# A two-block network on one core: the mixer's q matmuls by pairs of weight units, a stage's banks asked for one by one, and weight splits at fixed steps of a unit

## What is computed

```python
for l in range(DEPTH):
    x = layer_norm(ALPHA * x + 0.5 * swiglu(x, ffn1_w_gu[l], ffn1_w_down[l]), ln1_g[l], ln1_b[l])
    x = layer_norm(ALPHA * x + hybrid_mixer(x, w_in[l], ...), ln2_g[l], ln2_b[l])
    x = layer_norm(ALPHA * x + 0.5 * swiglu(x, ffn2_w_gu[l], ffn2_w_down[l]), ln3_g[l], ln3_b[l])

def hybrid_mixer(x, w_in, ...):
    z = x @ w_in
    sc_b, sc_c, sc_h, q, k, v, cc_a, cc_gate = jnp.split(z, IN_OFFSETS, axis=-1)
    y_sc = sc_b * depthwise_conv(sc_c * sc_h, sc_conv_w)            # 3 taps
    q = rope(q.reshape(b, s, 8, 64), positions)
    k = rope(k.reshape(b, s, 2, 64), positions)
    y_att = banded_window_attention(q, k, v, attn_sink)             # blocks of 128 tokens
    u = depthwise_conv(cc_a * jax.nn.sigmoid(cc_gate), cc_conv_w) + cc_conv_b   # 31 taps
    y_cc = jax.nn.silu(layer_norm(u, cc_ln_g, cc_ln_b))
    return jnp.concatenate([y_sc, y_att, y_cc], axis=-1) @ w_out
```

## Time and profile before

| | |
|---|---|
| median of three runs | 3479.86 us (3476.91 to 3484.40) |
| the profiled execution, its own time | 3478.07 us |
| its span, first to last instruction | 3476.3 us |
| mean granted TensorE clock | 0.986 |
| TensorE busy | 3324.5 us, 96% of the span |
| VectorE busy | 1725.2 us, 50% |
| ScalarE busy | 1097.7 us, 32% |
| weight loads | 514 of 512 KB, median 3.3 us from issue to landing |

### The profile page before, as it was taken

One profiled execution on the slowest core, in us unless ns is written; L12 is line 12 of the kernel. 1 busy time (PEld: TensorE's weight loads), 2 busy tenths in 40 slices (PEclk: granted clock), 3 DMA queues, 4 the chain that ended last, 5 costly groups with the idle time before them and its releaser, 6 DMA issues. The chain is left out here.

```text
span 3476.3 us, 42443 instructions
## 1 busy us (share of the span) xinstructions
PE 3324.5 (96%) x16776; PEld 2714.8 (78%) x16776; DVE 1725.2 (50%) x2526; ACT 1097.7 (32%) x1615; POOL 155.7 (4%) x204
## 2 busy tenths in 40 slices
PE   6999899989999999999999999999999999999999
PEld 5778777867777788778888768888888887678887
DVE  6655654456545553463333775332533337753334
ACT  4442223224432322333321343332233213433321
POOL 1000000001000000000000000000000001000000
PEclk9999999999999999999999999999999999999999
DMA  5222122232221111222332211333222322113232
GB/s 225 73 86 97 67 68 79 66 107 99 79 85 61 61 43 55 85 85 97 98 109 85 97 43 62 103 97 109 86 97 97 109 91 97 37 63 102 97 109 79
DMA packets 83494, 303.13 MB, mean 87 GB/s; under 512 B 9680, under 2 KB 9952, under 8 KB 83296
## 3 DMA queue, kind: packets, MB, share of 16 engines
q1 hardware_dynamic: 78064, 283.11, 24.1%
q0 software_dynamic: 5232, 17.31, 1.5%
HBM read 295.66 MB, written 4.72 MB: 86 GB/s over the span
## 5 line engine op out<-in xcount | busy, mean ns | idle before, releaser
L574 PE MATMUL bank<-hh,whi 128*128 128x512 f32 (+1 forms) x2704 | 1070.0, 396 | 26.4 <-DVE tmp L1210 8.4
L576 PE MATMUL bank<-hh,wlo 128*128 128x512 f32 (+1 forms) x2704 | 1029.3, 381 | 0.0
L575 PE MATMUL bank<-hl,whi 128*128 128x512 f32 (+1 forms) x2704 | 1027.1, 380 | 0.0
L1210 DVE TENSOR_TENSOR wlo<-raw,whi 128x1024 fp32r<-128x1024 f32 x498 | 610.4, 1226 | 757.7 <-ACT whi L2141 711.4
L2141 ACT CAST whi<-raw 128x1024 fp32r<-128x1024 f32 x498 | 523.4, 1051 | 731.4 <-PE bank L576 672.4
L574 PEld LDWEIGHTS bank<-hh,whi 128*128 128x128 f32 x2704 | 515.0, 190 | 155.0 <-issue 47.8
L576 PEld LDWEIGHTS bank<-hh,wlo 128*128 128x128 f32 x2704 | 514.1, 190 | 97.3
L575 PEld LDWEIGHTS bank<-hl,whi 128*128 128x128 f32 x2704 | 515.4, 191 | 80.1 <-issue 1.9
L574 PE MATMUL bank<-whi,fh 128*128 128x512 f32 x704 | 274.4, 390 | 0.0
L576 PE MATMUL bank<-whi,fl 128*128 128x512 f32 x704 | 273.9, 389 | 0.0
L575 PE MATMUL bank<-wlo,fh 128*128 128x512 f32 x704 | 273.9, 389 | 0.0
(11 more groups left out here) (321 smaller groups left out, 3708.8 us busy)
## 6 DMA issues: line engine op xcount, KB each, us to landing
raw<-in_W SPq DMA_DIRECT2D x514, 512.0 KB, 3.3
bc<-in_ln_g POOLq DMA_DIRECT2D x6, 512.0 KB, 4.1
bc<-in_ln_b POOLq DMA_DIRECT2D x6, 512.0 KB, 5.6
xn<-in_x SPq DMA_DIRECT2D x4, 512.0 KB, 8.7
mrg<-in_W SPq DMA_DIRECT2D x2, 1024.0 KB, 12.7
AR<-in_W SPq DMA_DIRECT2D x2, 1024.0 KB, 17.8
xn<-in_x POOLq DMA_DIRECT2D x4, 512.0 KB, 5.3
xd<-xn POOLq DMA_DIRECT2D x4, 512.0 KB, 3.6
```

The costliest lines, as they stand in the source:

```text
L574: e.matmul(out, ah, bh, start=first, stop=False, skip_group_check=True)
L575: e.matmul(out, ah, bl, start=False, stop=False, skip_group_check=True)
L576: return e.matmul(out, al, bh, start=False, stop=last, skip_group_check=True)
L1210: return self.e.tensor_tensor(o, a, b, op)
```

## The change

There are three edits.

1. `halves`: a unit's bank is asked for just before its first matmul in pass 0, not for all four ahead of the first.
2. `mixer`: the q matmuls go by two token tiles and two units: (t0,u0) (t0,u1) (t1,u0) (t1,u1), then (t0,u2) (t0,u3) (t1,u2) (t1,u3), then the same for tiles 2 and 3. Token tiles 2 and 3 of x are transposed after (t1,u1) and (t1,u2), rotated q of tiles 0 and 1 after (t3,u1) and (t3,u3).
3. VectorE and ScalarE set `paced` for the attention of the mixer.

```diff
@@ halves
-            jobs.append((key,) + self.coming(name, index, p) + (self.bank(self.all4, key),))
+            jobs.append((key,) + self.coming(name, index, p))
         for hf in range(2):
-            for n, (key, wh, wl, i, bank) in enumerate(jobs):
+            for n, (key, wh, wl, i) in enumerate(jobs):
+                bank = self.k.bank(key) if hf else self.bank(self.all4, key)
@@ TensorE.mixer
-        for t in range(4):
-            bank = self.bank(self.all4, ("q", l, t))
-            for u, (wh, wl, i) in enumerate(units):
...
-            if t < 2:
-                self.to_hT_tile(st, 2 + t)
-            else:
-                self.turn_q(l, t - 2)
+        for t, u in ((2 * tp + t, 2 * up + u) for tp in range(2) for up in range(2) for t in range(2) for u in range(2)):
+            wh, wl, i = units[u]
+            bank = k.bank(("q", l, t)) if u else self.bank(self.all4, ("q", l, t))
...
+            if t < 2 and (t, u) in ((1, 1), (1, 2)):
+                self.to_hT_tile(st, 1 + u)
+            elif t == 3 and u in (1, 3):
+                self.turn_q(l, u // 2)
@@ VectorE.mixer and ScalarE.mixer
+        self.paced = True
         mix(self.attention(l), side, 80, 78)
         drain(side)
+        self.paced = False
         self.project(4, st, ("ffn2", l), ...)
```

More of the change, by code:

```diff
@@ L1034, in mixer @@
                  for u in range(4)]
-        for t in range(4):
-            bank = self.bank(self.all4, ("q", l, t))
-            for u, (wh, wl, i) in enumerate(units):
[L1038 to L1043, removed]
-            if t < 2:
-                self.to_hT_tile(st, 2 + t)
-            else:
-                self.turn_q(l, t - 2)
+        for t, u in ((2 * tp + t, 2 * up + u) for tp in range(2) for up in range(2) for t in range(2) for u in range(2)):
+            wh, wl, i = units[u]
+            bank = k.bank(("q", l, t)) if u else self.bank(self.all4, ("q", l, t))
+            self.wait_ge(("hi", i), ("lo", i), ("hh", st, t, u // 2), ("hl", st, t, u // 2))
+            for j in range(2):
+                d = 2 * u + j
+                x = slice(512 * d + 128 * t, 512 * d + 128 * t + 128)
+                a = self.three(bank[:, :], k.hh[:, x], k.hl[:, x], HALF(wh, j), HALF(wl, j), d == 0, d == 7)
+            a.then_inc(*self.up(*([("used", i)] if t == 3 else []), *([("q", l, t)] if u == 3 else [])))
+            if t < 2 and (t, u) in ((1, 1), (1, 2)):
+                self.to_hT_tile(st, 1 + u)
+            elif t == 3 and u in (1, 3):
+                self.turn_q(l, u // 2)
         for n, _ in enumerate(self.conv_pair(l, 0), 1):
```

## The result

| | before | changed |
|---|---|---|
| median, us (lowest to highest) | 3481.0 (3476.91 to 3484.4) | 3459.46 (3453.43 to 3464.75) |
| ratio to before, 95% interval | | 0.9941, 0.9926 to 0.9955 |
| profiled execution: own time, span | 3478.07, 3476.3 | 3464.75, 3463.0 |
| TensorE busy, us; mean granted clock | 3324.5; 0.986 | 3320.3; 0.988 |

The account below looks back on a forecast made before the run. TensorE was taken as the bound, busy 3324.5 of 3476.3 us, so only its waits and half clock could be gained. -6.5 - 7.9 - 8.5 = -22.9 us gave 3455.2 for the profiled execution, 3457 as median, range 3446 to 3470.

Parts of the forecast that it names:

- part 1: Mixer's q in both layers: the new matmul order removes a 2.71 us weight wait and half clock, adds smaller waits; -6.5 us.
- rival 2: Clock drops at the waits left, the bank 3 wait in both mixers and ffn1 of layer 0: 3462 us, chance 0.15.
- -4.3: Sum for mixer 0's q, in us: -2.7 wait, -3.4 clock, +0.7 and +1.1 for two added waits.
- -7.7: Better bound for both mixers' q, in us, if the bank 3 wait stays at 1.14 and the first unit waits for nothing.
- Part 2: Banks one by one at stage starts: ffn1 of layer 1 -4.8, ffn1 of layer 0 -2.4, gated layer 1 -0.7; -7.9 us.
- Part 3: Splits at fixed steps in the attention: -11.5 us at its end, +3.0 in its middle; -8.5 us.
- The end: Attention's last `xl` wait: `acc` no longer behind a split, 4.9 us instead of 11.1 and 10.2; -11.5 us over both layers.
- The middle: Mid-attention `xl` wait grows from 2.43 to about 3.8 us with a clock drop: +3.0 us in layer 0, nothing in layer 1.
- Rival 1: The clock stays up in mid-attention, in layer 1 too: -6.0 us more, 3451 us, chance 0.2.
- Rival 3: End of the attention not released, ScalarE's chain having another cause than `acc`: the 11.5 us stay, 3468 us, chance 0.13.
- Rivals 4 and 5: 4: half clock lasts from mid-attention, 3514 us, chance 0.04. 5: attention ends when it did, 3472 us, chance 0.06.

Follow-up runs that it names:

- q alone: The kernel before with only the mixer's new q matmul order on TensorE: 3475.79 us, ratio 0.9989.
- rope: Changed kernel with VectorE's mixer order altered: first convolution unit split before tile 2's rotation, second behind it, tile 3 rotated before the other splits: 3451.0 us, ratio 0.9916.
- VectorE paced alone: Changed kernel with ScalarE's two `self.paced` lines taken out, so only VectorE's low halves stand at fixed steps: 3460.2 us, ratio 0.9944.
- pacing alone: The kernel before with only the splits at fixed steps in the attention, on VectorE and ScalarE: 3472.24 us, ratio 0.9976.
- the taps two steps later: Changed kernel with VectorE's convolution taps two steps later throughout the second half of the attention, same number in all: 3460.53 us, ratio 0.9941.
- the middle split behind its `xl`: Changed kernel with one VectorE split per layer moved from ahead of the mid-attention `xl` to three steps later, behind it: 3455.84 us, ratio 0.9932.
- pacing from block 6 on: Changed kernel with attention splits at fixed steps only from block 6 of 8 on, earlier blocks as in the kernel before: 3458.51 us, ratio 0.9939.

## Why the prediction was right

Direction, size and range came out: 21.5 us against 22.9. The stages of the two profiles give 20.1, as 4.0, 8.4 and 7.7 for the three parts; the forecast had 6.5, 7.9 and 8.5. So part 1 was 2.5 too large, and that the sum is nearer than this is in part luck. By its steps:

**Part 1, -6.5 forecast.** The waits were as worked out: 0.9 kept and 0.85 measured, 0.7 and 0.74, 2.2 and 2.08. The clock behind the first place held, as forecast. What the sum did not count, and rival 2 named, is the clock behind the new wait of 2.1: it fell in layer 0 of the changed kernel's profile, which made -4.3 into -2.3, and not in the run of q alone, where it was -3.8. With -1.8 in layer 1 (forecast -2.2) the part is 4.0 us in the one profile and 5.6 in the other; timed alone it is 3.8. The mis-sized term is the clock of layer 0, and not only for the new wait. The forecast took 3.4 us to be lost in the 7.0 us behind the old one, but TensorE was busy in 6.07 of them only the earlier trace rows, and half clock costs nothing while it waits: without its waits of over 0.2 us layer 0's q took 40.1 us before and 37.3 with q alone, 2.8 less. That is most of why q takes 42.0 us where the clock holds, in both layers, and not the 41.6 forecast. Of the bounds, -7.7 does not follow from its conditions: without the two new waits a layer is 1.8 us shorter, which makes -10.1 for two.

**Part 2, -7.9 forecast.** -2.2 and -4.5 in the two ffn1 (forecast -2.4 and -4.8), with the named releasers and 2.85 and 1.51 us (forecast 2.8 and 1.5). Gated 1 gave 1.7 in the profile where 0.7 was forecast. As a whole that stage says little: it takes 750.2 to 751.0 us in the three kernels without this edit and from 748.4 to 753.1 in the eleven with it. But its start, from the first transposes to those of x's tile 3, takes 26.0, 25.7 and 24.6 us without the edit and 23.9 to 24.1 in all eleven with it. The wait is 0.7 shorter, as forecast; the forecast left the half clock in, and against two of the three kernels without the edit some of it went as well (0.69 to 0.83 over 10 us in the windows above). Timed alone, the part is 8.4.

**Part 3, -8.5 forecast.** The end is right to a tenth: a wait of 0.84 for a forecast 0.9, 4.8 us of work and wait for 4.9, the clock up. ScalarE's chain moved by 1.9 us against the transposes, as worked out. The middle is right in its size, 3.74 for 3.8, +3.2 in layer 0 for +3.0; in layer 1 it is +0.7 for 0. The step that was too narrow there is "the split moves, but stays ahead of this `xl`. So TensorE waits just as long in sum": the two waits are 4.9 in sum, not 4.3, since the first stayed at 1.16. What holds is that this `xl` starts 65.0 us behind the first k/v matmul before and after. TensorE came to the middle earlier, as the wait of 0.71 at 1996.04 was gone, and waited there for what it had gained (0.6 of the 3.2 us; the rest is the clock). The forecast had neither that 0.7 in each layer nor what follows. Layer 1's attention took 147.0 us in the profile but 145.3 to 145.4 in three other kernels with the same order in it (rope, VectorE paced alone, and pacing alone); the 1.7 us are half clock in a stretch without a wait (the last one ahead of it, 1.29 us, had ended 1.5 us earlier, and stands in the other kernels too), which the windows of the changed kernel and then of the kernel with the mixer's order show over the same work:

```profile
3035.50:3040.50 5.00, 5.00 (x18) 3.42 (x16) 1.72 (x7) 4.85 (x8) 0.00 (x0) 0.66 0.33 105
```

```profile
3020.60:3025.60 5.00, 5.00 (x23) 3.17 (x21) 3.19 (x9) 4.86 (x8) 0.00 (x0) 1.00 0.32 105
```

**The rivals.** Rival 1 (the clock holds in mid-attention) did not come, in either layer. Rival 2 (it drops at what waits are left) came in one of its three places, the `qn` wait of layer 0, and not in ffn1 0. The rule cited there from the Trainium skill (TensorE: Matmul & The Clock Gate, Part 1: The HAM clock gate) names idling as what costs the clock; these runs agree that half clock stands mostly behind waits, but the same wait of 2.1 us cost it in one execution and not in another, and one stretch at 0.66 had none. Rival 3 fell with the last `xl` wait. Rivals 4 and 5 fell with the rows of the table: the attention got shorter by 3.8 and 3.9 us, and the stages behind it kept their length.

## What to carry to other kernels

When a helper engine in strict order has some work that is due now and some that is due a stage later, put the late work behind the urgent piece, and check it at each place: the same rule "at fixed steps" gained 6 us at the end of the attention and nothing up to its middle, where VectorE had no time to spare, and moving one split of 1.2 us there took 1.3 off the wait. Shifting a regular sequence of taps by a constant left the wait in the middle of it as it was and cost one at its end; and work drawn forward from a full stretch comes back as waits if the stretch before is full too. To judge a change of 0.6% from profiles, cut both at the same instructions: here the stages without a chance half clock repeat to a few tenths, where the whole span of one execution varies by 5.

## What was unexpected of the hardware

- The first 770 us, the same instructions in all 14 profiled kernels, took from 768.4 to 775.4 us. A part of it is the clock. Length times (1 - granted clock), added up over windows of 10 us from 20 to 790 us, is 10.2 us in the profile of the taps two steps later (768.7 us long), 13.7 in the kernel before (770.2), and 18.7 and 17.1 in the two longest, the changed kernel and the middle split behind its `xl` (775.3 and 775.4). It isn't all: the shortest, 768.4, has 15.3. What the rest is, and why the clock differs, is open.
- Half clock costs nothing where it lies ahead of a point that VectorE sets, or in TensorE's own waits. The pacing from block 6 on shows the first (142.5 us of attention with half clock ahead of `xl`, 142.5 in a layer without any), the term of 3.4 us in part 1, of which 2.8 came back, the second. I had priced such windows at their full length.
